# FF down projection of a two-block model as 16 units of seven block products, and conditioning rows spread over three stages

## What is computed

```python
# first block, after the mixers (w_ff1: 1024 x 4096, w_ff2: 4096 x 1024)
h2 = rmsnorm(x, g_mlp[l])
x = x + jnp.square(jax.nn.relu(h2 @ w_ff1[l])) @ w_ff2[l]
ple_gate = jax.nn.sigmoid(rmsnorm(x, g_ple[l]) @ w_ple_gate[l])
...
# second block (w_ada: 1024 x 6144; mod_c is used for its first two parts)
mod = (jax.nn.silu(c) @ w_ada[i] + b_ada[i]).reshape(B, N_ADA, D)[:, :, None, :]
mod_c = (jax.nn.silu(c_ctx) @ w_ada[i] + b_ada[i]).reshape(N_ADA, D)
```

## Time and profile before

| | |
|---|---|
| median of three runs | 3533.81 us (3530.88 to 3537.24) |
| the profiled execution's own time | 3534.49 us |
| its span, first to last instruction | 3532.7 us |
| instructions | 43926 |
| busy: PE, DVE, ACT, POOL | 96%, 64%, 45%, 23% |
| granted TensorE clock, mean | 0.987 |
| FF up, first to last matmul | 1256.75 to 1571.5 us |
| FF down | 1571.5 to 1926.25 us |

### The profile page before, as it was taken

How to read it: one execution, slowest core, us unless ns; L and a number is a source line. 1 busy time by engine, 2 the same in 40 slices (tenths; PEclk the granted TensorE clock), 3 DMA queues, 4 the chain that set the end, 5 groups by cost and what they waited for, 6 DMA issues and landing times.

```text
span 3532.7 us, 43926 instructions
## 1 busy us (share of the span) xinstructions
PE 3403.0 (96%) x17289; PEld 2803.6 (79%) x17289; DVE 2259.5 (64%) x2915; ACT 1575.2 (45%) x1946; POOL 799.2 (23%) x396
## 2 busy tenths in 40 slices
PE   7999999999999999999999999999896999999998
PEld 6667767667878878888888877777775999999997
DVE  4333445645447675666764854545756899999998
ACT  4344443234322343332213433433545677777776
POOL 3111111112212345544431221111222011101112
PEclk9999999999999999999999999999998999999999
DMA  5111113223465323336542241232633999999998
GB/s 201 49 48 54 66 54 103 78 96 131 160 216 184 101 87 117 117 137 223 203 158 71 81 158 65 81 119 98 191 124 151 389 379 378 388 385 385 380 379 311
DMA packets 131725, 626.75 MB, mean 177 GB/s; under 512 B 14849, under 2 KB 15241, under 8 KB 106690
## 3 DMA queue, kind: packets, MB, share of 16 engines
q1 hardware_dynamic: 126626, 606.12, 46.1%
q0 software_dynamic: 4752, 17.30, 1.8%
q10 hardware_dynamic: 144, 0.52, 0.0%
HBM read 520.67 MB, written 103.19 MB: 177 GB/s over the span
## 4 chain that ended last, share of the span: by engine, by line
PE 55%; DVE 6%; ACT 1%; issue 1%; DMA 1%; POOL 0%; POOLq 0%; DVEq 0%; SPq 0%; ACTq 0%
PE bank L268 8%; PE bank L270 7%; PE bank L269 7%; PE bank L3870 5%; PE bank L3869 5%; PE bank L3868 5%; PE bank L2123 3%; PE bank L2125 3%; PE bank L2124 3%; PE bank L3884 2%; PE bank L3885 2%; PE bank L3886 2%; DVE gqJ L2975 1%; PE bank L3855 1%; PE bank L2849 1%
## 5 line engine op out<-in xcount | busy, mean ns | idle before, releaser
L257 POOL TENSOR_TENSOR WL<-WR,WH 128x1024 fp32r<-128x1024 f32 (+1 forms) x177 | 400.6, 2263 | 1721.6 <-ACT WH L249 1718.5
L268 PE MATMUL bank<-XH,WH 128*128 128x512 f32 x1584 | 637.5, 402 | 10.0 <-ACT stg L553 5.0
L270 PE MATMUL bank<-XH,WL 128*128 128x512 f32 x1584 | 617.9, 390 | 0.0
L269 PE MATMUL bank<-XL,WH 128*128 128x512 f32 x1584 | 617.6, 390 | 0.0
L249 ACT ACTIVATE WH<-WR 128x1024 fp32r<-128x1024 f32 (+1 forms) x177 | 173.4, 979 | 511.4 <-PE bank L270 506.3
L3804 DVE TENSOR_TENSOR EL<-ER,EH 128x2816 fp32r<-128x2816 f32 x120 | 371.3, 3100 | 2.2 <-POOL warm L4095 2.2
L268 PEld LDWEIGHTS bank<-XH,WH 128*128 128x128 f32 x1584 | 297.8, 188 | 88.7 <-issue 15.9
L3799 ACT ACTIVATE EH<-ER 128x2816 fp32r<-128x2816 f32 x120 | 307.5, 2563 | 117.2 <-PE bank L3870 84.4
L269 PEld LDWEIGHTS bank<-XL,WH 128*128 128x128 f32 x1584 | 298.1, 188 | 64.7 <-issue 5.0
L270 PEld LDWEIGHTS bank<-XH,WL 128*128 128x128 f32 x1584 | 297.7, 188 | 62.9
L3868 PE MATMUL bank<-EH,WH 128*128 128x352 f32 x1024 | 336.2, 328 | 1.9 <-DVE WL L3992 1.9
(11 more groups left out here) (655 smaller groups left out, 6956.5 us busy)
## 6 DMA issues: line engine op xcount, KB each, us to landing
ER<-in_wu_dram SPq DMA_DIRECT2D x48, 1408.0 KB, 8.6
ER<-in_wd_dram SPq DMA_DIRECT2D x40, 1408.0 KB, 10.9
WR<-in_w_in_dram SPq DMA_DIRECT2D x89, 512.0 KB, 4.4
ER<-in_wg_dram SPq DMA_DIRECT2D x32, 1408.0 KB, 8.5
WR<-in_w_ff_dram SPq DMA_DIRECT2D x64, 512.0 KB, 4.7
aq<-in_w_ada_dram SPq DMA_DIRECT2D x48, 512.0 KB, 3.6
res<-in_wg_dram SPq DMA_DIRECT2D x16, 1408.0 KB, 8.0
res<-in_wu_dram SPq DMA_DIRECT2D x16, 1408.0 KB, 8.3
```

What stands on the lines that cost most here:

```text
L257: e.tensor_tensor(lo, raw, hi.bitcast(F32), ALU.subtract).then_inc(*w_lo.up("w_lo", n))
L268: e.matmul(bank[bk][:, 0:b - a], whi, xhi, start=k == 0, stop=False)
L269: e.matmul(bank[bk][:, 0:b - a], whi, xlo, start=False, stop=False)
L270: mm = e.matmul(bank[bk][:, 0:b - a], wlo, xhi, start=False, stop=k == K - 1)
```

## The change

**FF down becomes 16 more units** (n = 16 to 31) of the same form: `up_load`, `up_sum`, `up_hi`, `up_lo` now also serve the tiles of `w_ff2`, and one function `unit_pe` issues the matmuls of both halves (L2293 to L2295 after). Products 4 to 6 of a down unit run after products 0 to 3 of the next one.

**The factors.** The right operand, the hidden values, now needs factors T1 to T4 of its own. DVE makes them (`up_factor`, four subtractions of 512 a unit, L2011) as the up units run: T1 at the end of a unit, T3 and T2 at the head of the next, T4 after its first weight sum. Seven pieces of 256 KB are stored per unit in place of four, and read back in chunks of four units: seven factors of 1 MB (`down_load`), split in two halves of 1024 on ACT (`down_hi`) and on DVE (`down_lo`, L2208). At a change of chunk the low parts of factors 0 to 2 are made in the last unit of the old chunk, 3 to 6 in the first two units of the new one.

**The additions.** Of a down unit DVE does the operations that read a bank (L2549, L2553, L2554, L2569, L2585, L2605, L2621), POOL four additions into the residual from kept sums (`first_back`, `second_back`, `third_back`), ACT keeps the first product (`keep_first`). The squares for the next norm go through banks 6 and 7, the eight-bank rotation becoming six from unit 28 on; `ple` begins with half h=1.

**The conditioning rows** leave FF down. Rows 0 to 10 go to the beginning of the input projection, in five groups tied to the tiles' steps; rows 11 to 19 between the attention's `rope` and `values` steps; rows 20 to 47 (which need one vector) into the branch stage, two a tile in its first eight tiles, then one every second tile. The vectors come by broadcast loads of a new input row `crow` (L644 after), ACT's tanh (L648) and one DVE operation (L652), in place of ones-matmuls; a row is one instruction over 1024 in SBUF and a read of the accumulator (L659).

```diff
-        for t in range(32):
-            q, m = divmod(t, 8)
-            if t == 1:
...
-            for h in range(2):
-                bk = (2 * t + h) % 4
-                e.wait_ge(*on.bank(bk, "ff.ev", t, h))
-                gemm(e, N_FF + t, xs(T, DH[q % 2], DL[q % 2]), h * 512, h * 512 + 512, bk, h == 1,
+        for n in range(16, 33):
+            if n < 32:
+                for i in range(4):
+                    unit_pe(e, n, i)
+            if n > 16:
+                for i in range(4, 7):
+                    unit_pe(e, n - 1, i)
...
+    def down_lo(e, by, c, i):
+        for s in range(2):
+            e.wait_ge(*on("f.hi", c, i, s))
+            e.tensor_tensor(factor4_lo(i, s), factor4(i, False, s), factor4(i, True, s).bitcast(F32),
+                            ALU.subtract).then_inc(*by.up("f.lo", c, i, s))
...
+        if last:
+            down_lo(e, V, n // 4 - 3, 1)
+            sums(3)
+        sums(4)
...
+        if last:
+            down_lo(e, V, n // 4 - 3, 2)
+        sums(5)
...
+    ADA_EARLY, ADA_LATE, ADA_BR = ((0, 3), (3, 5), (5, 8), (8, 10), (10, 11)), 11, 20
...
+    def ada_rows(e, V, a, b, cs2, junk):
+        for x in range(a, b):
+            e.wait_ge(*on("ada", x))
+            for i in range(2 if x < 16 else 1):
+                e.wait_ge(*V.now)
+                e.tensor_tensor_reduce(junk, ada_raw(x), cs2[i], 0.5, pr("b_ada", x), ALU.mult, ALU.add,
+                                       mod[:, x, i:i + 1]).then_inc(*V.up("ada.ev", x, i))
...
+        for i in range(12, 16):
+            e.wait_ge(*on("p.out", i))
+        for i in range(2):
+            ada_cond_sp(e, i, ada_c[i], "crow")
+        ada_loads(e, 0, 3)
...
     def attention_act(e, st):
+        st.upto("ada", 0)
+        for i in range(2):
+            ada_cond_act(e, mla_act, i, ada_c[i], ada_t[i], "crow")
```

More of the change, by code:

```diff
@@ L652, in attention_pe @@
     def attention_pe(e, st):
+        for k in range(5):
+            st.until(2 * k + 2, "ada", k)
         st.until(12, "a0")
@@ new lines, in ff_sp @@
+        for i in (B21, T3, T2, T4):
+            up_store(e, 15, i)
+        down_load(e, 0, 6)
+        for n in range(16, 30):
+            if last_of_chunk(n):
+                for i in range(4):
+                    down_load(e, n // 4 - 3, i)
+            if n > 16 and first_of_chunk(n):
+                for i in (4, 5):
+                    down_load(e, n // 4 - 4, i)
+                up_load(e, n + 2, (0,))
+                down_load(e, n // 4 - 4, 6)
+                up_load(e, n + 2, (1,))
+            else:
@@ new lines, in ff_sq_act, with ff_sq_dve @@
+    def ff_sq_act(e, m, h):
+        q = 2 * m + h
+        e.wait_ge(*on("ff.res", m, h))
+        if q >= 4:
+            e.wait_ge(*on("ff.q_free", q - 2))
+        elif m:
+            e.wait_ge(*on(*SQ_FREE[h]))
+        e.activation(bank[6 + h][:, :] if m else acq[:, half(h)], xc(m)[:, half(h)], AF.Square).then_inc(
+            *ff_act.up("ff.sq", m, h))
+    def ff_sq_dve(e, *mh):
+        for m, h in mh:
+            e.wait_ge(*on("ff.sq", m, h))
+            if m > 1:
+                e.wait_ge(*on("ff.q_free", 2 * m + h - 2))
+            else:
+                e.wait_ge(*on("ff.sq", 0, h))
+            a = acq[:, half(h)]
+            e.tensor_tensor(a, a, bank[6 + h][:, :], ALU.add).then_inc(*ff_dve.up("ff.q_free", 2 * m + h))
+            on.at["ff.sum",] = on.at["ff.q_free", 2 * m + h]
@@ new lines, in down_act @@
+    def down_act(e, n):
+        before, c, last = n > 17 and first_of_chunk(n - 1), n // 4 - 4, last_of_chunk(n)
+        if before:
+            down_hi(e, c, 4)
+        keep_first(e, n)
+        if n == 16:
+            down_hi(e, 0, 4)
+        if before:
+            down_hi(e, c, 5)
+        up_hi(e, n + 1, 0)
+        if before:
+            down_hi(e, c, 6)
+        if n == 16:
+            down_hi(e, 0, 5)
+        up_hi(e, n + 1, 1)
+        if n == 16:
+            down_hi(e, 0, 6)
+        if n == 30:
+            for h in range(2):
+                ff_sq_act(e, 1, h)
+        up_hi(e, n + 1, 2)
+        if last:
+            down_hi(e, c + 1, 0)
+            down_hi(e, c + 1, 1)
+        up_hi(e, n + 1, 3)
+        if n == 30:
+            ff_sq_act(e, 2, 0)
+        up_hi(e, n + 1, 4)
+        if last:
+            down_hi(e, c + 1, 2)
+        if n == 30:
+            ff_sq_act(e, 2, 1)
+        up_hi(e, n + 1, 5)
+        if last:
+            down_hi(e, c + 1, 3)
+        if n == 29:
+            for h in range(2):
+                ff_sq_act(e, 0, h)
+        up_hi(e, n + 1, 6)
```

650 lines of the change are left out of this document (439 added, 211 removed).

## The result

The changed kernel takes 3554.68 us (median of five, 3550.6 to 3557.49) against 3533.81: a ratio of 1.0055, 95% interval 1.0044 to 1.0065. It is slower, by 21 us; 3516 was forecast, with a range from 3493 to 3540. The profiled execution took 3550.82 us, with a span of 3549.0, 16.3 more than before's; all that follows is counted in it.

A forecast was written before the change was run, and what follows sets the result against it. TensorE was taken to bound FF up and FF down. From the profiled 3534.49 us, -50.1 + 7.0 + 2.5 + 0.5 + 10 + 13.5 - 1.5 = -18.1 gave 3516 us, with an 8-in-10 range of 3493 to 3540.

The forecast's parts named there:

- FF down as units: FF down: 1344 matmuls in place of 1536, 304.6 us instead of 354.74 if nothing stalls, -50.1 us.
- Early rows: Input projection: rows delay ACT's emptying of bank 0 by 3.05 us and bank 1's by 3.9, together +7.0 us.
- Half clock: Input projection: the second stall, of 3.9 us, brings a window of PE at half clock, +2.5 us (0 to 3.4).
- Rows 11 to 19: Before the attention's first scores: 14 row operations, 19 us, fit mostly in DVE's idle time, 0 (to 4) us.
- Rows 20 to 47: Branch stage: at most two rows of 1.33 us a tile fit where DVE sits idle for 4.51 us, 0.
- Four factors a unit in FF up: FF up: DVE's unit grows to 18.65 us, under PE's 19.04, so PE isn't held, +0.5 us (0 to 1).
- rival B: FF up: DVE becomes the bound, 1.5 us a unit more than PE needs, 3545 us in all; chance 0.14.
- First change of chunk: Units 15 and 16: late low parts on DVE, with POOL beside it, stall PE by 5 to 16 us, +10 taken.
- Three later changes: FF down: loads in time, DVE's serial low parts late by 3.5, 5.5, 4 and 4 us; +13.5 us (3 to 25).
- Start of ple: Start of ple: the 1.48 us wait for the sum of squares is hidden by beginning with the other half, -1.5 us.
- Rival D: FF down: matmuls not saved; denied by count, half clock would double their cost after repeated idle near 3.87 us; no chance given.
- The rule on the shared port: SBUF: two-input VectorE and SBUF-reading GpSimd instructions exclude each other; 1.55 against 0.68 us; cited as speaking against the change.

The follow-up runs named there:

- early: Changed kernel with the next weight tile loaded ahead of vectors and first rows in the input projection, tanh and row groups one tile later: 3547.36 us.
- lag1: Changed kernel with each tile's row loads in the branch stage issued one tile later in SP's list: 3543.03 us.
- loads: Changed kernel with factors 0 and 1 loaded ahead of the second weight tile at the three later changes of chunk: 3550.54 us.
- best2: Changed kernel with early, lag1, loads, ordc, factor 6's high part later at the first chunk change, one row a tile in branch stage: 3532.02 us, 0.9989 against before.
- ordc: Changed kernel with ACT's high parts and DVE's low part of factor 3 moved earlier in their lists at the three later changes of chunk: 3552.44 us.

## Why the prediction was wrong, point by point

- **FF down as units, -50.1: right.** 1344 matmuls at 0.2267 us; the 40.5 us that did not come through are the changes of chunk (12.9 and 25.0) and 2.6 ahead of ple. Ordinary units of FF down take 19.04 us, so that they fit was right too (POOL has eleven operations in one, not the twelve that the prediction names once).
- **Early rows: right in mechanism, wrong in the clock.** 3.42 and 4.36 us stand where 3.05 and 3.9 were forecast, for the reasons named (a row operation is 1.36 us with its read, not 1.325). That the second came so near is in part luck. The row operation beside POOL's split took 2.0 us longer, which the sum did not hold, and the vectors came 1 us later; but PE too wanted the bank 2.7 us later (79.94, not 77.2), after a longer first stall and half clock. Half clock was sized from one window at 2.5 us; it was 6.0.
- **Rows 11 to 19: 0, measured +1.6,** inside the bound of 4. The same code took 0.2 to 0.4 us more than before in `early`, `lag1` and `loads`, so a cost is not shown.
- **Rows 20 to 47: 0. This step failed.** It looked at DVE's idle time and not at SP's queue: a row's load that waits for DVE stands ahead of the next weight tile's. It cost 12.0 us; lag1 takes back 8.8 with SP's order alone, and best2, with one row a tile besides, all but 0.9. The prediction counted what the rows add to DVE, and did not follow their loads through the queue in which the weight loads stand.
- **Four factors a unit in FF up: right that PE is not held, wrong in DVE's length.** From the third unit on every one is 19.04 us long; rival B falls. DVE is busy for 18.1 to 18.7 us of a unit only while it is late, near the 18.65 forecast for every unit. In settled units it is 15.0, and it waits for PE's banks again, so the 2.7 us of lag forecast for the last unit are not there. (The 14.96 us that the sum began from also hold 1.24 us of waiting.)
- **First change of chunk: +10, measured 12.9,** with waits of 0.5, 3.6 and 1.2 us for DVE's low parts as forecast and one of 3.66 for POOL's low part of a weight sum, which was not. The idle time, 9.0, is near the 10 partly by luck: DVE's low parts held PE for 5.3.
- **Three later changes: +13.5, measured 25.0. The second step that failed.** The range (3 to 25) held it at its end. Idle time is 17.0 us of it, in waits for DVE's low parts of the size that was named (5.0, 6.6 and 5.4, where 3 to 6 was); the rest is half clock and the matmuls around the waits, which this term did not have. The step that failed is the one that put POOL's additions at nothing: they fit in an ordinary unit, and in the last unit of a chunk they are what the changes cost, 3.7 us when they are cut to 8 columns (small), 13.8 when DVE does them (dveb). Nor were "the loads in time": they stood in SP's queue behind a weight load that waited for POOL. How much of that goes through the loads and how much through the stretched low parts stays open.
- **Start of ple: -1.5, measured 0 to the end.** The wait of 1.48 us is gone, but half clock and two waits of 0.38 and 0.29 us at ple's beginning take its place. Besides, PE waits 2.40 us ahead of ple's first matmul, which the table counts in FF down, by the profile for a kept sum on DVE (L2605):

```profile
1942.53 0.50 PE L267 MATMUL bank<-YH,WH 128*128 128x512 f32 x1 [2.40 <-DVE XLf L2605]
```

- **Half clock** is the term that was mis-sized most: 6.0, 3.2 and 8.2 us in the three stretches, 17.4 in all and none in before, against 2.5. Rival D had it in a clause and gave it no price.
- **The rule on the shared port.** The Trainium skill ("SBUF — State Buffer", Who interferes with whom) lets a VectorE instruction with two SBUF inputs and a GpSimd instruction that reads SBUF run only one after the other. The trace agrees: 4.09 and 4.02 us for pairs of low parts that take 2.36 alone, 3.29 for a row operation of 1.28. The prediction cited it against the change and then let POOL's additions through because an ordinary unit fits.

The sign was wrong because three terms were too small at once: the branch stage by 12.0 us, the three changes by 11.5, half clock at the beginning by 3.5. Rival B, the only slower case, was none of them.

## What to carry to other kernels

Of work that is moved, follow its transfers through the queue that they are put into: a load that waits for a late consumer holds every load behind it, and the weight tile of the next product may be one of them. Give each stall a second price for the clock behind it, read from a row of this kernel. And where two engines share the burst at a change of buffers, take work off the one that both the other engine and the queue wait for before reordering anything. Two reorderings of loads and lists here won nothing that can be told from the scatter; moving POOL's four additions to DVE took the three changes from 25.0 us to 13.8 in one run and to 18.4 in another with the same lists there. Before reading a gain of a few us, look what the same code took in another run.

## What was not expected of the hardware

The prediction took an idle time of 3.04 us as harmless and one of 3.87 as not the earlier trace rows. The runs do not bear out such a border. Windows here give PE's busy time and matmuls, PEclk, DMA share and GB/s. In before, full clock follows the wait of 3.04 us:

```profile
759.40:766.20 6.80, 6.80 (x30) 1.00 0.69 231
```

In ordc the same place of the program waits as long, and half clock follows (PE's timeline and a window of it):

```profile
772.61 0.50 PE L267 MATMUL bank<-XH,WH 128*128 128x512 f32 x1 [3.01 <-ACT stg L546]
```

```profile
774.10:777.40 3.30, 3.30 (x9) 0.50 1.00 315
```

In early PE is at full clock without a gap from 87 to 116.6 us and then at half for 3.3 (two windows):

```profile
116.70:120.00 3.30, 3.30 (x9) 0.50 0.18 74
87.00:116.60 29.60, 29.60 (x127) 1.00 0.53 181
```

Before has no half clock there. PE's busy time hides what it did. From 113.35 to 115.3 us it ran four matmuls of one row each (L708, 1x512 out), and in nine of the thirteen changed runs half clock begins 2.0 to 3.3 us behind the first of these four. In the other four, and in before, it does not, so what sets it off at that place stays open. Within after, a wait of 3.56 us at 1692.23 comes with 6.8 us of half clock, one of 3.57 at 1777.87 with none, one of 2.23 at 1069.79 with 3.4. What the runs show is a sum: in after some 44 us stood at half clock between 57 us and ple's first matmuls, in before 6.8.
